# Opening roundings in another order, and the scores of three MLA heads in other PSUM banks

## The reference: what is computed

```python
for l in range(DEPTH):                       # 2
    h = _rmsnorm(x, attn_norm[l])
    proj = jnp.einsum('bsd,de->bse', h, w_in[l])
    (d_q, d_k, d_v, g_q, g_k, g_v, g_r, g_o, m_qa, m_kva, m_kr) = _split_cols(proj, IN_SPLIT_SIZES)
    ...                                      # A: differential attention, 6 heads
    ...                                      # B: gated linear attention (GLA), 4 heads
    mq = jnp.einsum('bsr,re->bse', _rmsnorm(m_qa, mla_q_norm[l]), mla_w_q_b[l])
    mkv = jnp.einsum('bsr,re->bse', _rmsnorm(m_kva, mla_kv_norm[l]), mla_w_kv_b[l])
    ...                                      # C: multi-head latent attention (MLA), 6 heads
    o_mla = _causal_attention(mq, mk, mv, (MLA_NOPE + MLA_ROPE) ** -0.5)
    mixed = jnp.concatenate([o_diff, o_gla, o_mla], axis=-1)
    x = x + jnp.einsum('bse,ed->bsd', mixed, w_out[l])
    h2 = _rmsnorm(x, ffn_norm[l])
    ff = jax.nn.silu(h2 @ w_gate[l]) * (h2 @ w_up[l])
    x = x + ff @ w_down[l]
return _rmsnorm(x, final_norm)
```

## Time and profile before

| | |
|---|---|
| median of three runs | 2243.1 us (2242.52 to 2243.57) |
| the profiled execution | 2243.08 us, span 2241.3 us |
| PE busy | 2213.9 us, 99% of the span |
| DVE busy | 1277.8 us, 57% |
| ACT busy | 948.5 us, 42% |
| mean granted TensorE clock | 0.997 of full |
| HBM read | 399.54 MB, 179 GB/s over the span |

### The profile page before, as it was taken

One profiled execution on the slowest core, in us unless ns is written; L12 is line 12 of the kernel. 1 busy time (PEld: TensorE's weight loads), 2 busy tenths in 40 slices (PEclk: granted clock), 3 DMA queues, 4 the chain that ended last, 5 costly groups with the idle time before them and its releaser, 6 DMA issues.

```text
span 2241.3 us, 27415 instructions
## 1 busy us (share of the span) xinstructions
PE 2213.9 (99%) x11060; PEld 1890.2 (84%) x11060; DVE 1277.8 (57%) x1371; ACT 948.5 (42%) x963; POOL 24.0 (1%) x24
## 2 busy tenths in 40 slices
PE   8999999999999999999999999999999999999998
PEld 6899988888888888888888999888888888888886
DVE  4576774555555555455655866745555455555555
ACT  5454543533333333333453645444333333333333
POOL 0000000000000000000000000000000000000000
PEclk9999999999999999999999999999999999999999
DMA  6544455555555555555555434555555555555554
GB/s 220 182 146 128 133 178 188 175 192 192 191 187 187 191 191 192 191 188 188 188 184 171 146 109 155 174 184 188 188 189 190 191 193 192 187 188 189 194 192 155
DMA packets 221095, 402.67 MB, mean 180 GB/s; under 512 B 13377, under 2 KB 53601, under 8 KB 220897
## 3 DMA queue, kind: packets, MB, share of 16 engines
q1 hardware_dynamic: 220304, 400.90, 54.6%
q10 hardware_dynamic: 720, 0.78, 0.1%
HBM read 399.54 MB, written 2.10 MB: 179 GB/s over the span
## 4 chain that ended last, share of the span: by engine, by line
PE 97%; DMA 1%; DVE 1%; issue 1%; ACT 1%; SPq 0%; POOLq 0%; POOL 0%; ACTq 0%; DVEq 0%
PE bank L600 29%; PE bank L602 29%; PE bank L601 29%; PE bank L576 2%; DMA stage<-in_w_in 1%; PE bank L725 1%; PE bank L954 0%; PE bank L952 0%; PE bank L953 0%; PE bank L666 0%; PE bank L789 0%; PE bank L777 0%; PE bank L667 0%; PE bank L668 0%; PE bank L676 0%
## 5 line engine op out<-in xcount | busy, mean ns | idle before, releaser
L1297 DVE TENSOR_TENSOR w_lo<-stage,w_hi 128x2048 fp32r<-128x2048 f32 (+4 forms) x398 | 861.7, 2167 | 707.7 <-ACT w_hi L991 706.8
L991 ACT ACTIVATE w_hi<-stage 128x2048 fp32r<-128x2048 f32 (+4 forms) x398 | 721.5, 1815 | 959.0 <-DMA stage<-in_w_down 307.5
L600 PE MATMUL bank<-w_hi,xt_hi 128*128 128x512 f32 (+4 forms) x2336 | 880.7, 377 | 11.3 <-DVE w_lo L1297 6.0
L602 PE MATMUL bank<-w_hi,xt_lo 128*128 128x512 f32 (+4 forms) x2336 | 871.4, 373 | 0.0
L601 PE MATMUL bank<-w_lo,xt_hi 128*128 128x512 f32 (+4 forms) x2336 | 870.8, 373 | 0.0
L600 PEld LDWEIGHTS bank<-w_hi,xt_hi 128*128 128x128 f32 x2336 | 439.6, 188 | 85.4 <-issue 12.7
L602 PEld LDWEIGHTS bank<-w_hi,xt_lo 128*128 128x128 f32 x2336 | 439.5, 188 | 69.4
L601 PEld LDWEIGHTS bank<-w_lo,xt_hi 128*128 128x128 f32 x2336 | 440.0, 188 | 68.2
L600 PE MATMUL bank<-w_hi,f_hi 128*128 128x512 f32 x640 | 249.1, 389 | 0.0
L602 PE MATMUL bank<-w_hi,f_lo 128*128 128x512 f32 x640 | 249.0, 389 | 0.0
L601 PE MATMUL bank<-w_lo,f_hi 128*128 128x512 f32 x640 | 249.0, 389 | 0.0
(11 more groups left out here) (207 smaller groups left out, 1214.4 us busy)
## 6 DMA issues: line engine op xcount, KB each, us to landing
stage<-in_w_gate SPq DMA_DIRECT2D x176, 512.0 KB, 4.3
stage<-in_w_up SPq DMA_DIRECT2D x176, 512.0 KB, 4.4
stage<-in_w_down SPq DMA_DIRECT2D x174, 512.0 KB, 4.5
stage<-in_w_in SPq DMA_DIRECT2D x96, 384.0 KB, 3.7
stage<-in_w_out SPq DMA_DIRECT2D x64, 512.0 KB, 4.3
stage<-in_w_in SPq DMA_DIRECT2D x54, 512.0 KB, 4.6
stage<-in_w_in SPq DMA_DIRECT2D x16, 320.0 KB, 3.5
stage<-in_w_q_b SPq DMA_DIRECT2D x12, 384.0 KB, 3.7
```

Source lines behind the costliest of these rows:

```text
L600: pe.matmul(acc, a, wh[:, i, :], start=first and i == 0, stop=False)
L602: mm = pe.matmul(acc, b, wh[:, i, :], start=False, stop=last and i == len(kts) - 1)
L991: act.activation(w_hi[s][:, 0:kts * cols], stage[s][:, 0:kts * cols], ACT.Copy).then_inc(hi_made[s], 1)
L1297: vec.tensor_tensor(w_lo[s][:, 0:kts * cols], stage[s][:, 0:kts * cols], w_hi[s][:, 0:kts * cols].bitcast(F32), ALU.subtract).then_inc(lo_ ...
```

## The change

It has two parts that do not touch each other.

**The opening.** Unit 1 is now also loaded, rounded and waited for in pieces, two of 1024 columns (two kt) each (`PIECES`). The transfers are the same two, in the same place of SP's queue. ACT and DVE handle unit 3 in block c = 2, ahead of the last two rounds of the activations, and the main loop's step 0 rounds nothing in layer 0. PE's unit 0 runs through each kt in three passes over both token tiles: high by high, which waits for `first_hi` and `xt_hi_made` alone; then the low weights, which wait for `first_lo`; then the low activations, which wait for the bank's `bank_free`.

**The scores' banks.** The scores of MLA heads 0 to 5 go to the banks 4, 5, 5, 6, 6, 6 in place of bank 6 throughout. What reads them on DVE follows. Heads 0, 1 and 2 are those of the steps 32, 33 and 34.

```diff
+PIECES = [(0, k, 1) for k in range(4)] + [(1, 0, 2), (1, 2, 2)]
+SCORE_BANK = [4, 5, 5, 6, 6, 6]
...
-            "head_scores": lambda j: [6] if j < MLA_HEADS else [6, 7], "head_turn": lambda _: [4],
+            "head_scores": lambda j: [SCORE_BANK[j]] if j < MLA_HEADS else [6, 7], "head_turn": lambda _: [4],
...
-            return quad + 1 - (n % 4 == 0)
+            return quad + 1 - (n % 4 < 2)
...
+            def load_piece(i):
+                n, k, m = PIECES[i]
+                rows_ = slice((4 * n + k) * P, (4 * n + k + m) * P)
+                sp.dma_start(stage[n][:, k * NCH:(k + m) * NCH].rearrange("p (k n) -> p k n", k=m),
+                             w_in[0, rows_, C_QA:C_QA + NCH].rearrange("(k p) n -> p k n", p=P)).then_inc(first_in[i], 16)
...
+                    if layer == 0 and n == 1:
+                        load_piece(4)
+                        load_piece(5)
+                        continue
...
-                    opening = layer == 0 and n == 0
+                    opening = layer == 0 and n < 2
...
+                        if opening and n == 0:
+
+                            pe.wait_ge(first_hi, i + 1)
+                            pe.wait_ge(xt_hi_made, kt + 1)
+                            for t in range(NT):
+                                pe.matmul(bank[2 * parity + t][:, 0:cols], hi[:, at, t * P:(t + 1) * P], wh[:, i, :],
+                                          start=i == 0, stop=False)
+                            pe.wait_ge(first_lo, i + 1)
+                            for t in range(NT):
+                                pe.matmul(bank[2 * parity + t][:, 0:cols], hi[:, at, t * P:(t + 1) * P], wl[:, i, :],
+                                          start=False, stop=False)
+                            copied((norm, kt // 2), norm_bank(layer, norm, kt // 2))
+                            for t in range(NT):
+                                mm = pe.matmul(bank[2 * parity + t][:, 0:cols], lo[:, at, t * P:(t + 1) * P], wh[:, i, :],
+                                               start=False, stop=False)
+                            continue
+                        if opening and i % 2 == 0:
+                            pe.wait_ge(first_lo, 5 + i // 2)
...
-                        ps = bank_taken(key, 6)
+                        ps = bank_taken(key, SCORE_BANK[j])
...
-                        mm.then_inc(bank_full[6], 1)
+                        mm.then_inc(bank_full[SCORE_BANK[j]], 1)
...
-                        if c < 2:
+                        if c == 0:
+                            round_first(4)
+                            round_first(5)
+                        elif c < 3:
                             round_unit(0, c + 1)
...
-                    if n < U_FF - LEAD + 1:
+                    if (1 if layer == 0 else 0) <= n < U_FF - LEAD + 1:
                         round_unit(layer * QUADS + (n + LEAD) // 4, n + LEAD)
```

More of the change, by code:

```diff
@@ L370, in program @@
         full = [sem(f"full{s}") for s in range(4)]
-        first_in = [sem(f"first_in{k}") for k in range(4)]
+        first_in = [sem(f"first_in{k}") for k in range(len(PIECES))]
         warm_made = sem("warm_made")
@@ L456, in load_x @@
                 sp.dma_start(resid[:, :, part], x[:, part].rearrange("(t p) d -> p t d", p=P)).then_inc(x_in[c], 16)
+            def load_piece(i):
[3 more added lines that the diff above has]
+                             w_in[0, rows_, C_QA:C_QA + NCH].rearrange("(k p) n -> p k n", p=P)).then_inc(first_in[i], 16)
             load_x(0)
-            for k in range(4):
-                sp.dma_start(stage[0][:, k * NCH:(k + 1) * NCH], w_in[0, k * P:(k + 1) * P, C_QA:C_QA + NCH])\
-                    .then_inc(first_in[k], 16)
+            for i in range(4):
+                load_piece(i)
             def load(quad, n, sources, second_first=False):
@@ L589, in unit @@
                         hi, lo, at = operand(kt)
-                        if opening:
-                            pe.wait_ge(first_lo, i + 1)
                         if i == 2 and midway:
                             norm_turn(norm, midway)
+                        if opening and n == 0:
[15 more added lines that the diff above has]
+                            pe.wait_ge(first_lo, 5 + i // 2)
                         if norm and kt % 2 == 0:
@@ L991, in round_unit, with round_first @@
                 act.activation(w_hi[s][:, 0:kts * cols], stage[s][:, 0:kts * cols], ACT.Copy).then_inc(hi_made[s], 1)
[L993 to L996, removed]
+            def round_first(i):
+                n, k, m = PIECES[i]
+                part = slice(k * NCH, (k + m) * NCH)
+                act.wait_ge(first_in[i], 16)
+                act.activation(w_hi[n][:, part], stage[n][:, part], ACT.Copy).then_inc(first_hi, 1)
             for layer in range(DEPTH):
@@ L1303, in _, with rest_of_first @@
                 vec.memset(mx[:, i:i + 1], 0.0).then_inc(free, 1)
[L1305 to L1308, removed]
+            def rest_of_first(i):
+                n, k, m = PIECES[i]
+                part = slice(k * NCH, (k + m) * NCH)
+                vec.wait_ge(first_hi, i + 1)
+                vec.tensor_tensor(w_lo[n][:, part], stage[n][:, part], w_hi[n][:, part].bitcast(F32), ALU.subtract)\
                    .then_inc(first_lo, 1)
@@ L1378, in opening @@
                             norm_lo("norm1", [2 * c, 2 * c + 1], 0)
-                        if c < 2:
+                        if c == 0:
+                            rest_of_first(4)
+                            rest_of_first(5)
+                        elif c < 3:
                             rest_of_unit(0, c + 1)
@@ L1580, in head_scores @@
                     mla = j < MLA_HEADS
-                    for branch in range(1 if mla else 2):
-                        ps = masked_bank_in(("head_scores", j), 6 + branch)
+                    banks = [SCORE_BANK[j]] if mla else [6, 7]
+                    for branch, bank_of in enumerate(banks):
+                        ps = masked_bank_in(("head_scores", j), bank_of)
                         for t in range(NT):
@@ L1587, in head_scores @@
                                                            mx[:, k:k + 1])
-                        ins.then_inc(bank_free[6 + branch], 1)
-                    for b in (6,) if mla else (6, 7):
+                        ins.then_inc(bank_free[bank_of], 1)
+                    for b in banks:
                         copied(("head_scores", j), b)
```

## The result

The changed kernel takes 2230.6 us (median of five runs, 2230.3 to 2232.38) against 2243.28 us of the kernel before, a ratio of 0.9946 with a 95% interval of 0.9934 to 0.9958. The busy times and PE's waits of the changed kernel answer to the earlier trace rows; in its listing line 631 is the old 600, 1332 the old 1297, 1393 the old 1357.

A forecast was written before the change was run, and what follows sets the result against it. PE bounds the kernel, busy 2213.9 of 2241.3 us, so gains come only from its idle time or half-clock matmuls. 4.01 + 1.65 + 0.86 + 0 + 3.9 = 10.4 us off 2243.1 gives 2232.7, range 2231.2 to 2236.8.

The forecast's parts named there:

- likeliest case: Whole kernel: the opening's and the scores' gains all arrive, 2232.7 us, chance 0.60.
- The start of unit 1: Opening: rounding the first half early shortens the chain to PE; gain 0.86 us, start 18.76 to about 17.9.
- Unit 3's wait and its clock: Ahead of and in unit 3: PE's 4.01 us wait goes, and 1.65 us of half clock with it.
- The scores: MLA scores: six PE waits for the mask copies go; gain 3.9 us, bounds 0 and 4.5.
- rival 2: Banks 4 and 5: `head_out(0)` or a transpose waits for the scores as long as before; 2236.6 us, chance 0.05.
- The start of unit 0: Opening: PE begins about 1.4 us earlier, lengthening idle time ahead of unit 1; value 0, bounds 0 and loss of 1.65.
- two cases: Unit 0: half clock as before, then 1.7 us idle; or clock kept up, 3.1 us idle and possibly 1.65 lost.
- rival 1: Ahead of unit 1: the clock falls after 3.1 us idle, costing 1.65; 2234.35 us, chance 0.24.
- Behind the opening: After unit 3: everything comes 6.5 us earlier and loads move with PE; cost nothing, at worst all 6.5 lost.
- rival 3: Behind the opening: weight transfers set the pace, leaving only the scores' gain; 2239.2 us, chance 0.06.
- The sum: Whole kernel: 4.01 + 1.65 + 0.86 + 0 + 3.9 = 10.4 us, giving 2232.7 us.

The follow-up runs named there:

- without the passes: Changed kernel with unit 0's matmuls in the old order, waiting for first_lo: 2230.9 us, ratio 0.9947.
- scores alone: Kernel before with only the scores' banks changed to 4, 5, 5, 6, 6, 6: 2238.01 us, ratio 0.9978.
- filling the gap: Changed kernel with eight more matmuls into bank 3 between unit 0 and unit 1's first wait: 2230.30 us, ratio 0.9946.
- unit 3 alone: Kernel before with only unit 3's rounding moved on ACT and DVE to block c = 2: 2236.48 us, ratio 0.9971.
- passes alone: Kernel before with only unit 0's three passes as in the change: 2245.06 us, ratio 1.0007.

## Why the prediction was wrong

Its direction, its mechanisms and its likeliest case held; its size did not, and the range was cut too close below. By its own steps:

- *The start of unit 1*: right. Half the rounding took 1.06 us (1.05 estimated), unit 1 started 0.84 us earlier (0.86), and the ACTq issues moved with it.
- *Unit 3's wait and its clock*: right in kind, 5.95 in place of 5.66. The step said 4.01, "4.0 at most". That is the idle time as the profile names it, from the modelled end of one matmul to the start of the next; from start to start unit 3 came 4.16 late (35.73 less 31.57, where the next matmul was due, one step of 0.23 behind the one at 31.34). The clock's part was 1.76 in place of 1.65: unit 3 takes 5.44 us at full clock (36.14 less 30.70), where the step had taken 5.55 from other matmuls. ACT's and DVE's order left the cover that was worked out: no wait for low weights stands there.
- *The scores*: the mechanism was right and the term mis-sized, 3.9 for 4.65. The text gave 4.5 as the upper bound with the reason in it and still took the named sum. The Trainium skill ("Perfetto Trace Analysis", Tensor Engine Instruction) says that TensorE's ends are estimated and not observed; the runs fit that, since a wait named 0.40 costs 0.66. No wait came back at `head_out` (rival 2).
- *The start of unit 0*: value 0 was right in the median. Of its two cases the second came, in which the clock stays up: unit 0's matmuls kept the full clock, and PE was idle 2.95 and 2.98 us (3.1 worked out). Its bound, a loss of 1.65, was too small: the fall costs 1.4 us in one profile and 2.9 in another kernel's. That no gain was possible hung on unit 0's end at 17.39, and in two profiles of the old order (without the passes, and the scores alone) unit 0's last matmul starts 1.4 and 1.6 us later, since its half clock lasts longer there. The clock fell ahead of unit 1, as rival 1 has it, in one of the changed kernel's two profiles and, by their times, perhaps in two more of its ten runs.
- *Behind the opening*: right, -0.08 us; units and loads moved together (rival 3 did not come).
- *The sum*: this is the step that failed. It took the end of the execution to move with PE. The span also has 10.4 us behind PE's last matmul, and these shrank by 0.84, because the change puts one more instruction into DVE's stream: DVE's extra instruction alone does the same to the kernel before, ACT's does not. I had looked at what that instruction costs and not at what it displaces.

Together: +0.29 at unit 3, +0.75 at the scores, +0.84 at the end and -0.1 elsewhere make 1.8 us, the difference between the 10.4 and the 12.2 of a profile pair without a fall. The scores' 0.75 or the end's 0.84 alone would have left the time inside the range (2230.6 + 0.8 = 2231.4); the two together put it below. The medians differ by 12.7 in the first series and 12.3 in the second; the last few tenths are within the spread of runs and were not traced.

## What to carry to other kernels

Price a wait on PE from start to start of its matmuls, in the kernel without the wait where one can be had; the idle time that the profile names was short by 0.07 to 0.26 us each, a fifth of the sum over six small waits. An earlier start ahead of a wait that stays is not neutral: it moves idle time into one piece, and a long piece of idle time can cost clock, 1.4 or 2.9 us here. Leaving the work late, or filling the gap, showed no such run in five each. For effects under 0.1% read what lies behind the last matmul as well, since an edit at the front can change it.

## What the runs showed of the hardware

- PE idle for 3.0 us at the same place cost the clock in some executions of one kernel and not in others: 1.00 in the profile of 2230.86 us, 0.56 and 0.72 in that of 2232.38. Of the five profiles with such a stretch ahead of unit 1, four show the fall. Idle stretches of 1.2 to 1.4 us ahead of unit 1 did not cost it; those of 3.9 and 4.0 us did in every profile taken, and so did those of 1.9 to 2.7 us ahead of unit 0, in all seven profiles with its old order.
- A fall at the same place has two sizes: from unit 1's first matmul to unit 3's it is 12.78 us without one, 14.15 and 14.19 with the short one, 15.69 in two profiles with the long one.
- A transfer of 8 KB of instructions, in the middle of the last output store, goes with a landing of 4.0 us in place of 3.1: in all five kernels whose profile shows the late transfer (before, scores alone, unit 3 alone, passes alone, ACT's extra instruction), and in none of the eight others. Whether the store waits for the transfer itself was not tried.
